# Compressed keys and the first unit's scores set between the last query tiles, with the gates' tile first

## What is computed

```
proj  = rmsnorm(h) @ w_q                     # 16 query heads and 48 gate columns
q     = proj[..., :2048];  gates = sigmoid(proj[..., 2048:])
# compression branch: 32 rows of raw keys (or values) become one, every 16 rows
first  = einsum('bnjche,cjef->bnchf', sub + pe[:16], cmp_w1[:, :16])
second = einsum('bnjche,cjef->bnchf', sub + pe[16:], cmp_w1[:, 16:])
hid    = gelu(first[:, :-1] + second[:, 1:] + cmp_b1)
ckv    = einsum('bnchf,cfe->bnche', hid, cmp_w2)
# per head: softmax(q k / sqrt(128) + bias) v for each branch, gated and summed, then @ w_o
```

## Time and profile before

| | us |
|---|---|
| median of three runs (2542.59 to 2543.60) | 2542.88 |
| profiled execution, its time | 2544.02 |
| profiled execution, its span from first to last instruction | 2542.4 |
| PE busy | 2492.3 (98%) |
| DVE / ACT / POOL busy | 1197.2 / 923.1 / 268.2 |
| mean granted clock of TensorE | 0.996 |

### The profile page before, as it was taken

The page is one execution under the profiler, slowest core; times in us unless marked ns, Lnnn a source line. Parts: engine busy times, 40 slices in busy tenths (PEclk is TensorE's granted clock), DMA queues, the critical chain, the costliest instruction groups (busy, mean ns, idle before and its releaser), DMA issues.

```text
span 2542.4 us, 44214 instructions
## 1 busy us (share of the span) xinstructions
PE 2492.3 (98%) x17440; PEld 2459.0 (97%) x17440; DVE 1197.2 (47%) x1354; ACT 923.1 (36%) x1158; POOL 268.2 (11%) x316
## 2 busy tenths in 40 slices
PE   7999999999999999999999999999999999999997
PEld 7899999999999999999998899999999999999997
DVE  7564444444444444653535744744444444444444
ACT  5554233323323333532325733633233323323332
POOL 0420000000000001300002411300000000000012
PEclk9999999999999999999999999999999999999999
DMA  6444444344444444446445564344444444444443
GB/s 249 167 141 149 152 165 149 136 164 165 149 146 167 148 148 153 144 151 177 162 177 192 175 195 149 116 149 156 158 149 150 157 157 150 153 155 157 150 147 130
DMA packets 89739, 400.67 MB, mean 158 GB/s; under 512 B 13788, under 2 KB 24940, under 8 KB 60114
## 3 DMA queue, kind: packets, MB, share of 16 engines
q1 hardware_dynamic: 78066, 377.82, 43.6%
q0 software_dynamic: 6160, 12.60, 1.5%
q10 hardware_dynamic: 5456, 9.52, 1.1%
HBM read 392.16 MB, written 19.02 MB: 162 GB/s over the span
## 4 chain that ended last, share of the span: by engine, by line
PE 90%; DVE 4%; ACT 3%; issue 1%; DMA 1%; SPq 0%; ACTq 0%; POOL 0%; DVEq 0%
PE ps L1467 28%; PE ps L1469 28%; PE ps L1468 28%; PE ps L1568 2%; ACT w_hi L524 1%; DVE w_lo L875 1%; ACT y L631 0%; ACT x_hi L549 0%; DMA rowsK<-cmp_data_dram 0%; PE ps L1594 0%; DMA pastV<-win_kv_dram 0%; PE ps L1787 0%; ACT sq L557 0%; DVE ps L917 0%; DVE x_lo L893 0%
## 5 line engine op out<-in xcount | busy, mean ns | idle before, releaser
L1467 PE MATMUL ps<-x_hi,w_hi 128*128 128x320 f32 x3536 | 1094.9, 310 | 5.5 <-DVE sg L1096 2.5
L1468 PE MATMUL ps<-x_lo,w_hi 128*128 128x320 f32 x3536 | 1093.1, 309 | 0.0
L1469 PE MATMUL ps<-x_hi,w_lo 128*128 128x320 f32 x3536 | 1093.1, 309 | 0.0
L875 DVE TENSOR_TENSOR w_lo<-w_raw,w_hi 128x2048 fp32r<-128x2048 f32 (+1 forms) x362 | 744.5, 2057 | 648.5 <-ACT w_hi L524 648.3
L524 ACT CAST w_hi<-w_raw 128x2048 fp32r<-128x2048 f32 (+1 forms) x361 | 617.1, 1710 | 506.8 <-PE ps L1469 474.8
L1467 PEld LDWEIGHTS ps<-x_hi,w_hi 128*128 128x128 f32 x3536 | 664.2, 188 | 7.7 <-DVE sg L1096 3.0
L1468 PEld LDWEIGHTS ps<-x_lo,w_hi 128*128 128x128 f32 x3536 | 664.2, 188 | 0.4 <-issue 0.2
L1469 PEld LDWEIGHTS ps<-x_hi,w_lo 128*128 128x128 f32 x3536 | 664.1, 188 | 0.0
L1467 PE MATMUL ps<-hid_hi,w_hi 128*128 128x320 f32 x1408 | 435.1, 309 | 0.0
L1469 PE MATMUL ps<-hid_hi,w_lo 128*128 128x320 f32 x1408 | 435.1, 309 | 0.0
L1468 PE MATMUL ps<-hid_lo,w_hi 128*128 128x320 f32 x1408 | 435.1, 309 | 0.0
(11 more groups left out here) (267 smaller groups left out, 1454.4 us busy)
## 6 DMA issues: line engine op xcount, KB each, us to landing
w_raw<-w_in_dram SPq DMA_DIRECT2D x176, 1024.0 KB, 4.9
w_raw<-w_out_dram SPq DMA_DIRECT2D x128, 704.0 KB, 4.0
w_raw<-w_kv_dram SPq DMA_DIRECT2D x24, 1024.0 KB, 6.5
w_raw<-w_q_dram SPq DMA_DIRECT2D x17, 1024.0 KB, 5.0
w_raw<-w_o_dram SPq DMA_DIRECT2D x15, 1024.0 KB, 5.5
win_out_dram<-win_kv_dram POOLq DMA_DIRECT2D x8, 992.0 KB, 5.3
rowsK<-cmp_data_dram SPq DMA_DIRECT2D x16, 256.0 KB, 9.1
pastK<-slc_k_dram SPq DMA_DIRECT2D x16, 256.0 KB, 3.2
```

What stands on the lines that cost most here:

```text
L875: V.tensor_tensor(w_lo[:, slot, 0:width], src, w_hi[:, slot, 0:width].bitcast(F32), ALU.subtract).then_inc(lo_made, 1)
L1467: M(out, wh, xh[:, k, :], start=(k == 0), stop=False)
L1468: M(out, wh, xl[:, k, :], start=False, stop=False)
L1469: last = M(out, wl, xh[:, k, :], start=False, stop=(k == kt - 1))
```

## The change

The tile of the gates becomes the first of the projection; head u is now tile `P_Q + 1 + u`. The sigmoid, the gates' transposes on PE and their folding on DVE follow right behind tile `P_Q + 1`. The keys' weights `w1Kp` are now the load behind the last panel (region Z), and the values' weights `w1Vp` the later one. The raw keys are copied to a buffer of their own, `rowsPK`, early in the projection. On PE the keys' 32 products (64 by halves of the rows) stand behind tile `P_Q + 13`, the turn of their sums behind tile `P_Q + 14`, their last product inside tile `P_Q + 15` (before step 12), and the scores of unit 0 between tiles `P_Q + 15` and `P_Q + 16`. The values' part stays behind the last tile. Units use PSUM banks 2 and 3 first, then 0 and 1. `biasP` is waited for by halves. ACT runs the exponentials of unit 0 between the two gelus.

```diff
+        panel(P_Q, 0, w_q[NH], PW)
+        section(P_Q + 1, NH, w_q, PW)
         sp.wait_ge(trow_sum, 1)
-        sp.dma_start(w1Vp[:, :, :], cmp_w1[1]).then_inc(w1Vp_in, 16)
+        sp.dma_start(w1Kp[:, :, :], cmp_w1[0]).then_inc(w1Kp_in, 16)
...
         sp.wait_ge(lo_made, P_WO)
-        sp.dma_start(w1Kp[:, :, :], cmp_w1[0]).then_inc(w1Kp_in, 16)
+        sp.dma_start(w1Vp[:, :, :], cmp_w1[1]).then_inc(w1Vp_in, 16)
...
+        sp.wait_ge(tile_made, P_WO - 1 + TOFF)
+        bias_half(0)
         load_keys(0)
+        sp.wait_ge(tile_made, P_WO + TOFF)
+        bias_half(1)
...
+        with pe.Fori(1, NH // 2 - 1) as i:
+            for j in range(2):
+                tile(P_Q + j, i, KT, x_hi, x_lo)
+        pe.wait_ge(w1Kp_in, 16)
+        pe.wait_ge(rowsPK_made, 1)
+        crow_rows(0, w1Kp, rowsPK)
+        tile(P_Q + NH - 2, 0, KT, x_hi, x_lo)
+        turn_sums(0, crowK)
+        tile(P_Q + NH - 1, 0, KT, x_hi, x_lo, compressed_keys)
...
+        pe.wait_ge(kc_made, 2)
+        scores(0)
+        tile(P_Q + NH, 0, KT, x_hi, x_lo)
+        pe.wait_ge(w1Vp_in, 16)
+        turn_values(0)
+        turn_values(1)
+        pe.wait_ge(rowsPV_made, 1)
+        crow_rows(1, w1Vp, rowsPV)
+        turn_sums(1, crowV)
...
+            if s == 0:
+                dve.wait_ge(tile_made, P_WO + TOFF)
+                V.tensor_copy(rowsPV[:, :].rearrange("p (v t) -> p v t", v=NKV), kv_c[:, NKV:2 * NKV, 0:SEQ]).then_inc(rowsPV_made, 1)
+                scaled(P_Q + NH, 0, qT[:, NH - 1, :])
+                sample_bias()
+                compressed_bias(1)
+                crow_copy(1, crowV)
+                recips(0)
+                cmp_join(3, C_BANK[1], NKV, False)
```

More of the change, by code:

```diff
@@ L207, in build @@
     hcP = at("hcP", "S", [P, 2, NKV * NCMP])
+    turn_at = at.used["S"]
+    crowK = at("crowK", "S", [P, 2 * P])
+    at.used["S"] = turn_at
     vCP = at("vCP", "S", [P, NKV * HD])
@@ L751, in _ @@
         hi_split(P_Q + 1, 0)
+        act.wait_ge(bank_read[P_Q % 2], (P_Q + TOFF) // 2 + 1)
+        A(gT[:, :], gT[:, :], ACT.Sigmoid).then_inc(sig_made, 1)
+        nc.scalar.copy(rowsPK[:, :].rearrange("p (v t) -> p v t", v=NKV), kv_c[:, 0:NKV, 0:SEQ]).then_inc(rowsPK_made, 1)
         with act.Fori(0, NH // 2 - 1) as i:
@@ L755, in _ @@
         hi_split(P_Q + NH, 0)
[L756 to L759, removed]
+        gelu(2, 0, hcP[:, 0, :])
         def copy_vP(n):
@@ L767, in copy_vP, with prompt_values @@
             nc.scalar.copy(vP[:, n // 2, n % 2, :], ps[:, 4 + n, :]).then_inc(vt_made, 1)
[L769 to L776, removed]
+        def prompt_values():
+            copy_vP(0)
+            copy_vP(1)
+            gelu(3, 1, hcP[:, 1, :])
+            copy_vP(2)
+            copy_vP(3)
+            act.wait_ge(kc_sum, 3)
+            nc.scalar.copy(vCP[0:NCMP, :], ps[0:NCMP, 4, :]).then_inc(vcp_made, 1)
         def exps(p):
@@ L1186, in _, with crow_copy @@
         lo_split(P_Q + 1, 0)
[L1187 to L1205, removed]
+        def crow_copy(c, dst):
+            dve.wait_ge(crow_sum, c + 1)
+            V.tensor_copy(dst[:, :], ps[:, C_BANK[c], 0:2 * P]).then_inc(crow_made, 1)
+        scaled(P_Q, 0, gT[:, :])
+        lo_split(P_Q + 2, 0)
+        scaled(P_Q + 1, 0, qT[:, 0, :])
+        lo_split(P_Q + 3, 0)
         dve.wait_ge(g_sum, 1)
@@ L1214, in _ @@
                         ALU.add).then_inc(gates_made, 1)
+        V.tensor_tensor(fold[:, :], ident[:, 0:NSEQ], ident[:, NSEQ:2 * NSEQ], ALU.add).then_inc(fold_made, 1)
         dve.wait_ge(gates_made, 1)
[L1218 to L1231, removed]
+        with dve.Fori(0, NH // 2 - 3) as i:
+            for j in range(2):
+                scaled(P_Q + 2 + j, i, qT[:, i * 2 + 1 + j, :])
+                lo_split(P_Q + 4 + j, i)
+        scaled(P_Q + NH - 4, 0, qT[:, NH - 5, :])
+        lo_split(P_Q + NH - 2, 0)
+        scaled(P_Q + NH - 3, 0, qT[:, NH - 4, :])
+        lo_split(P_Q + NH - 1, 0)
+        crow_copy(0, crowK)
+        scaled(P_Q + NH - 2, 0, qT[:, NH - 3, :])
+        lo_split(P_Q + NH, 0)
+        cmp_join(2, C_BANK[0], NKV, False)
         dve.wait_ge(kc_sum, 2)
@@ L1234, in _, with compressed_bias, sample_bias @@
                       ps[:, 3, 0:NKV * NCMP].rearrange("p (v s) -> p v s", v=NKV)).then_inc(kc_made, 1)
+        scaled(P_Q + NH - 1, 0, qT[:, NH - 2, :])
+        dve.wait_ge(mask_set, 1)
+        def compressed_bias(n):
+            rows = slice(bias_at(n * (NH // 2)), bias_at(n * (NH // 2)) + NH // 2)
+            dve.wait_ge(bias_in[n], 16)
+            V.tensor_copy(biasC[:, 1, rows, :], biasP[:, rows, CB - 1:SEQ:CS])
+            n0 = len(range(P + CB - 1, SEQ, CS))
+            V.tensor_copy(biasC[:, 0, rows, 0:n0], biasP[:, rows, P + CB - 1:SEQ:CS]).then_inc(bias_made, 1)
+            dve.wait_ge(bias_made, n + 1)
+        def sample_bias():
+            dve.wait_ge(mask_set, 2)
+            dve.wait_ge(bias_s_in, 16)
+            V.tensor_copy(bias_n[:, DB - 1, :], bias_s[:, PAST:PAST + DS])
+            for v in range(NKV):
+                rows = slice(32 * v, 32 * v + 32)
+                last = V.tensor_copy(biasSC[rows, v * NCMP:(v + 1) * NCMP], bias_s[rows, CB - 1:PAST:CS])
+            link(last)
+        compressed_bias(0)
         def scores_p(p):
-            u, s3, a = unit(p), p % 3, 2 * (p % 2)
+            u, s3, a = unit(p), p % 3, score_bank(p)
             dve.wait_ge(s_made, p + 1)
```

99 lines of the change are left out of this document (46 added, 53 removed).

## The result

The changed kernel has a median of 2554.99 us (2553.98 to 2559.24, 5 runs) against 2543.49 us (2542.59 to 2545.2, 5 runs) for the kernel before beside it: a ratio of 1.0043 with a 95% interval of 1.0032 to 1.0054. It is slower, by 11.5 us of the medians. The profiled execution has a span of 2553.2 us against 2542.4, so +10.8. Predicted were 2551.2 us, that is +8.3, with a range of 2546.5 to 2556.

What follows compares the result with a forecast made beforehand. TensorE was taken as the bound, with only 3.3 us of waits to win. The terms -3.3 + 7.7 + 1.7 + 1.1 + 0.3 + 0.8 = +8.3 us, added to 2542.88, gave 2551.2 us, range 2546.5 to 2556.

Steps and rivals of the forecast that it cites:

- the four old waits: TensorE's waits for unit 0's softmax, the keys' gelu, their copy and their sums' copy: all gone, -3.3 us.
- wait for w1Kp: Behind tile 13, TensorE waits for the keys' weights, loaded behind the last panel: +7.7 us, low end 5.8.
- the clock's fall: Behind the pause for w1Kp, TensorE's granted clock falls once: +1.7 us, ends 0 and 3.4.
- wait for rowsPV: Behind tile 16, TensorE waits for DVE's raw values' copy, queued behind unit 0's bias: +1.1 us, 0 to 2.2.
- wait for crowV: TensorE waits for DVE's copy of the values' sums, behind biasP's second half: +0.3 us, 3.3 if that half takes 8.3.
- outputs of unit 0 (pT): TensorE's outputs of unit 0 are delayed by ACT's table load ahead of unit 1's exponentials: +0.8 us, 0 to 1.3.
- What is removed: Same matmuls, four TensorE waits gone for -3.3 us; early gates' work taken as free on ACT and DVE.
- The rival of weights that are there in time: The keys' weights land before TensorE asks, so no wait or clock fall: -1.1 us, 2541.8 us; chance 0.08.
- The rival of a wait without a fall: TensorE waits for w1Kp but the clock stays full: +6.6 us, 2549.5 us; chance 0.21.
- Waits behind the last tile: Behind tile 16, TensorE waits 1.1 us for the raw values' copy and 0.3 us for the values' sums' copy.
- ACT's tables: Exponentials between the gelus make ACT load two more tables of 1.28 us; cost to TensorE 0 to 1.3, taken 0.8.

Runs made afterwards that it cites:

- repaired: load_early_dve_order plus another bank order for units' scores, a later bank wait, and transposes ahead of the values' sums' turn; 2543.83 us, ratio 0.9992 to the kernel before.
- load_one_panel_early: The changed kernel with the load of w1Kp issued one panel earlier, between the last two panels; 2547.02 us, ratio 1.0007 to the kernel before.
- copy_first: load_early with DVE's copy of unit 0's transposed probabilities (pT) ahead of unit 2's bias and maxima; 2547.12 us, ratio 1.0008 to the kernel before.
- warm_whole_wait: The changed kernel with 33 filler products on constants in front of TensorE's wait for w1Kp; 2556.46 us, ratio 1.0044 to the kernel before.
- load_early: The changed kernel with the load of w1Kp issued right behind the gates' panel, ahead of the other sixteen; 2546.54 us, ratio 1.0007 to the kernel before.
- products_one_tile_later: The changed kernel with the keys' products behind tile 14, their sums' turn and copy later too, load unmoved; 2548.98 us, ratio 1.0011 to the kernel before.
- load_early_dve_order: load_early with DVE's raw values' copy and last scaling ahead of unit 0's bias, second bias half behind the join; 2546.34 us, ratio 1.0003 to the kernel before.

## Why the prediction was right, and where its sizes were off

The sum of the trace, made as the prediction made its own, is -3.3 + 7.5 + 1.9 + 2.1 + 0.7 + 0.7 + 1.4 = +11.0 us, against +10.8 in the region.

| term | predicted | measured |
|---|---|---|
| the four old waits | -3.3 | -3.3 |
| wait for w1Kp | +7.7 (low end 5.8) | +7.5 |
| the clock's fall | +1.7 (0 to 3.4) | +1.9 |
| wait for rowsPV | +1.1 (0 to 2.2) | +2.1 |
| wait for crowV | +0.3 (up to 3.3) | +0.7 |
| wait for the join of the values' sums (sub) | not in the sum | +0.7 |
| outputs of unit 0 (pT) | +0.8 (0 to 1.3) | +1.4 |
| sum | +8.3 | +11.0 |

The same account holds in the other kernels if the pastV wait is added, and the clock where it fell: repaired has 1.4 - 3.3 + (0.8 - 1.6) = -2.7 against -3.1 measured, load_one_panel_early 5.4 - 3.3 + (0.7 - 1.6) = +1.2 against +0.9, copy_first 4.7 - 3.3 + (3.0 - 1.6) + 1.7 = +4.5 against +4.3. With it the change itself comes to 11.0 + (2.0 - 1.6) = +11.4 against +10.8. Such sums come out 0.2 to 0.6 us above the region, so terms of that size and below aren't resolved.

**What is removed: right.** All four waits of the earlier trace rows went. The early gates cost nothing that shows: from 1230 to 1326 us TensorE waits once, for 0.3 us, before the change and after it. repaired bears the 3.3 us out: with one new wait of 1.4 us left and 0.8 less for pastV, the waits make the region 2.7 us shorter than before, and it is 3.1 shorter. In the change they are gained, and more than paid back by the 4.9 us of small new waits behind tile 16.

**The new wait for w1Kp: right, and shown.** 7.7 was worked out as the load's time less the 2.4 us that the queue leaves it. Measured are 9.5 us to landing (10.1 was taken) and a lead of 2.05, so the wait is 7.5: two misses of 0.6 and 0.35 us that partly cancel. load_one_panel_early is the test of the working: 7.35 us more lead, 0.4 more to landing, 7.0 us less wait. The rival of weights that are there in time falls with it.

**The clock: right in size, wider in kind.** 1.7 was read from the stretches behind other pauses at the kernel's start, 0.78, 0.50 and 0.87 over 2 us each; 1.9 came, so the size was carried over and not worked out. The rival of a wait without a fall is wrong. warm_whole_wait shows that the pause is the cause. What the prediction didn't see is that the second pause, of 2 us, can be followed by a fall as well. It reasoned that the wait of 2.2 us had left the clock at 1.00, which was one case; with a pause of 2.0 us load_early lost it (0.84, 0.50, 0.80) and with 2.1 load_one_panel_early didn't. With the pause of 7.5 us the clock fell (0.68 and 0.57); behind pauses of about 2 us the runs show both, a fall and none.

**Waits behind the last tile: right in place, too small.** The wait for rowsPV is 1.0 us above the sum's term, and two sizes made it. With E, the end of tile 15, at 1354.28, where unit 0's scores start, the prediction had the first half of biasP landing at E + 7.3 and the copy done at E + 10.8, while TensorE wants it at E + 9.7. The 2 MB ahead of the half were issued 3.2 us before E and not 3.7, and the half landed 7.9 us after its own issue, at E + 8.1. Bias, maxima and the copy took a little less than worked out, and the copy was done at E + 11.4, 0.6 late. TensorE was ready at 1365.78 - 2.07, E + 9.4, 0.3 early. The order of DVE's work is as predicted:

```profile
1362.45 0.27 DVE L1245 COPY biasC<-biasP 128x120 f32<-128x120 f32 x1 [7.47 <-DMA biasP<-bias_rows]
...
1364.44 0.68 DVE L1281 TENSOR_REDUCE neg<-sc 128x2 f32<-128x512 f32 x1
1365.04 0.68 DVE L1347 COPY rowsPV<-kv_c 128x1024 f32<-128x1024 f32 x1
...
1368.38 0.30 DVE L1245 COPY biasC<-biasP 128x120 f32<-128x120 f32 x1 [1.40 <-DMA biasP<-bias_rows]
...
1369.61 0.42 DVE L1207 COPY crowV<-ps 128x256 f32<-128x256 f32 x1 [0.79 <-PE ps L1708]
...
1371.24 1.06 DVE L1053 TENSOR_TENSOR sub<-sub 128x60 f32<-128x60 f32 x1
```

The wait is thus near its upper end of 2.2. For crowV the mechanism was wrong: in the change DVE isn't held by the second half of biasP when the values' products end, it waits 0.79 us for them. By the prediction's own sum the half would have cost nothing once rowsPV took 2.1 us: the sums out 6.2 us behind the tile, TensorE ready at 6.9. What the sum put at nothing is the way from the last product through DVE's copy back to TensorE, with no other matmuls between: that is the 0.7 us. The prediction's mechanism does exist: products_one_tile_later shows it, with 3.2 us. The join's wait (sub) is a term that the prediction left out. Unit 1's scores need the bank that the values' sums are joined from, and the join is done 0.7 us after TensorE has come there. repaired shows the place: with the banks in another order and transposes as cover, both waits are gone.

**ACT's tables: right that the outputs of unit 0 wait, half right in the reason.** The two more table loads are there. The gelus (L577, at 1348.77 and 1370.68) and the exponentials (L801) load twice each in this stretch, where each loaded once before:

```profile
1352.00 1.28 ACT L801 ACT_TABLE_LOAD   x1
...
1370.68 1.28 ACT L577 ACT_TABLE_LOAD   x1
...
1377.61 1.28 ACT L801 ACT_TABLE_LOAD   x1
1378.90 0.35 ACT L801 ACTIVATE sc<-sc,neg 128x60 f32<-128x60 f32 x1
```

The last one does stand ahead of unit 1's exponentials, which end at 1380.43, and DVE's reciprocals of unit 1 need them:

```profile
1380.46 0.18 DVE L1311 RECIPROCAL rec<-tot 128x3 f32<-128x3 f32 x1
```

Behind these comes the copy of pT that TensorE waits 1.4 us for. But DVE's maxima of unit 2, which stand ahead of the reciprocals, end only at 1380.35, so without the load the copy could have been about 0.1 to 0.2 us earlier (an estimate from these two ends). The prediction left out DVE's order, unit 2 ahead of the copy. With that changed, in copy_first, TensorE waits 0.7 us for ACT's half of the copy, and there the load is on the chain: it stands from 1369.74 to 1371.02, and from it to the copy at 1372.47 ACT has no gap. Each load is 1.28 us, as in the earlier trace rows, and the exponentials start 0.01 us behind the last one (1377.61 + 1.28 against 1378.90).

**The forecast.** The sum was 2.7 us too small: 1.0 for rowsPV, 0.4 for crowV, 0.7 for the join, 0.6 for pT and 0.2 for the clock, less 0.2 for w1Kp. The 1.4 us for pT lie above the end of 1.3 that the prediction gave that term, and the join was in no term at all. The profiled pair moved by 10.8 and the medians by 11.5, and the kernel before had 2543.49 in the runs beside it, 0.6 above the 2542.88 that the prediction started from. So 2554.99 lies 1 us below the range's upper end. The two large terms, which make the direction and most of the size, are right by their mechanism; that the small misses, nearly all on one side and one of them in no term, still stayed inside the range is in part luck. What I would do otherwise is to write, for each wait that a reorder makes, the round trip between the engines and the bank that the next work needs.

## What to carry to other kernels

A load behind the last panel of the stream needed its whole landing time in lead here: when a user is moved ahead, ask where on the queue its load was, and work out how many panels ahead it has to go. One panel here, 7.35 us of lead for a load of 9.5 to 9.9, was the difference between 7.5 and 0.5 us. And a reorder that removes four small waits has to be read again with each engine's queue in hand, since DVE's order, a shared bank and an uncovered round trip gave back more (4.9 us) than was gained (3.3 us).

## What was unexpected of the hardware

- A pause of about 2 us in dense work was sometimes followed by a fall of the clock and sometimes not. It fell behind 2.00 us (load_early: 0.84, 0.50, 0.80, and 5.38 us for products that take 3.69) and behind 2.17 us (copy_first, pastV: 0.81, 0.50, 0.84). It stayed at 1.00 behind 1.83 (copy_first), 1.97 and 2.07 (the change), 2.03 (warm_whole_wait), 2.08 (load_one_panel_early) and 2.17 us (the kernel before). What decides it is open. In load_early_dve_order it fell behind two waits of 0.7 and 1.1 us, within 3 us of each other, with none of 2 us near. Behind all five pauses of 2.6 to 7.5 us in the region it fell (7.47, 3.29, 3.24, 2.67, 2.56).
- Taking a long pause away didn't free the part behind it: in load_early and warm_whole_wait a fall stood behind a later pause. In load_one_panel_early and repaired none came from 1326 to 1400. With one trace of each, it isn't shown that one fall's absence causes the next.
- A matmul of fillers on 128x128 took 4.40 / 38 = 0.116 us in the projection, so that 19 filler steps, of two matmuls each in the trace, took 4.40 us and not the 7.0 I had expected from the same call elsewhere in the kernel.
- With unchanged code, the part behind the region varied between 1072.5 and 1075.9 us over the ten kernels' profiled executions. Differences of a microsecond or two in the whole span say nothing here about a single edit; the region does.
